# First FFN of a two-layer trunk: 18 of its 22 gate and up pairs by one level of Strassen's scheme

## The reference

```python
def swiglu_ffn(x, norm_g, w_gate_up, w_down):
    gate, up = jnp.split(rms_norm(x, norm_g) @ w_gate_up, 2, axis=-1)
    return x + (jax.nn.silu(gate) * up) @ w_down
```

## Time and profile before

| | |
|---|---|
| median of three runs | 1491.09 us (1486.75 to 1492.95) |
| the profiled execution | 1486.6 us, span of its instructions 1484.9 us |
| TensorE matmuls / weight loads | busy 1431.6 us (96%) / 1336.6 us (90%) |
| VectorE, ScalarE, GpSimd | busy 879.9 us (59%), 646.4 us (44%), 159.4 us (11%) |
| granted TensorE clock, mean | 0.991 of 2.4 GHz |
| read from HBM | 134.73 MB |

### The profile page before, as it was taken

One profiled execution on the slowest core, in us unless ns is written; L12 is line 12 of the kernel. 1 busy time (PEld: TensorE's weight loads), 2 busy tenths in 40 slices (PEclk: granted clock), 3 DMA queues, 4 the chain that ended last, 5 costly groups with the idle time before them and its releaser, 6 DMA issues.

```text
span 1484.9 us, 29208 instructions
## 1 busy us (share of the span) xinstructions
PE 1431.6 (96%) x11504; PEld 1336.6 (90%) x11504; DVE 879.9 (59%) x1562; ACT 646.4 (44%) x1086; POOL 159.4 (11%) x194
## 2 busy tenths in 40 slices
PE   7999988898999999999999999999998999999998
PEld 6999987887899999999999967755698999999998
DVE  6887556667984444443223426466577999997222
ACT  5444532333443443433222364556655655555111
POOL 1000022202630000000111000253110000000000
PEclk9999989999999999999999999999999999999999
DMA  5222200002444223233322322265521333233322
GB/s 219 86 85 85 74 12 30 29 30 87 156 149 141 86 85 99 86 98 106 92 83 97 113 62 85 74 196 159 171 85 58 98 102 105 93 113 107 91 91 83
DMA packets 48588, 144.79 MB, mean 98 GB/s; under 512 B 6912, under 2 KB 16224, under 8 KB 47344
## 3 DMA queue, kind: packets, MB, share of 16 engines
q1 hardware_dynamic: 42048, 118.57, 25.0%
q0 software_dynamic: 6160, 20.79, 4.7%
q10 hardware_dynamic: 288, 4.19, 0.7%
HBM read 134.73 MB, written 7.76 MB: 96 GB/s over the span
## 4 chain that ended last, share of the span: by engine, by line
PE 81%; DVE 10%; issue 5%; ACT 3%; DMA 1%; DVEq 0%; ACTq 0%; POOLq 0%
PE PS L610 67%; PE PS L1317 4%; PE PS L1318 4%; PE PS L1319 4%; DVE arena L2164 2%; ACT arena L1825 1%; PE PS L1143 1%; DVE arena L2327 1%; DVE mx L2602 1%; DVE arena L2154 0%; DVE arena L2159 0%; ACT wsplit L1376 0%; ACT wsplit L1450 0%; DVE wsum L1996 0%; DVE arena L2379 0%
## 5 line engine op out<-in xcount | busy, mean ns | idle before, releaser
L610 PE MATMUL PS<-xnh,wsplit 128*128 128x260 f32 x2496 | 410.8, 285 | 12.8 <-DVE wsplit L1932 12.4
L610 PEld LDWEIGHTS PS<-xnh,wsplit 128*128 128x128 f32 x2496 | 346.7, 190 | 15.7 <-DVE wsplit L1932 13.1
L1376 ACT ACTIVATE wsplit<-wring 128x1024 fp32r<-128x1024 f32 x132 | 136.3, 1033 | 326.0 <-PE PS L610 323.7
L1932 DVE TENSOR_TENSOR wsplit<-wring,wsplit 128x1024 fp32r<-128x1024 f32 x132 | 157.1, 1190 | 172.9 <-ACT wsplit L1376 172.8
L610 PE MATMUL PS<-xnl,wsplit 128*128 128x260 f32 x1248 | 252.2, 284 | 0.0
L610 PEld LDWEIGHTS PS<-xnl,wsplit 128*128 128x128 f32 x1248 | 193.3, 189 | 0.0
L610 PE MATMUL PS<-arena 128*128 128x128 f32 (+9 forms) x1104 | 170.9, 322 | 13.1 <-DVE arena L2327 8.6
L1317 PE MATMUL PS<-movh,wsplit 128*128 128x260 f32 x616 | 176.2, 286 | 6.3 <-ACT rinv L1496 2.8
L610 PEld LDWEIGHTS PS<-arena 128*128 128x128 f32 (+2 forms) x1104 | 134.3, 191 | 48.3 <-issue 30.1
L1319 PE MATMUL PS<-movh,wsplit 128*128 128x260 f32 x616 | 174.3, 283 | 0.0
L1318 PE MATMUL PS<-movl,wsplit 128*128 128x260 f32 x616 | 174.2, 283 | 0.0
(11 more groups left out here) (451 smaller groups left out, 2245.6 us busy)
## 6 DMA issues: line engine op xcount, KB each, us to landing
wring<-in_w_gu SPq DMA_DIRECT2D x88, 512.0 KB, 3.5
wring<-in_w_dn SPq DMA_DIRECT2D x32, 512.0 KB, 3.5
wring<-in_w_proj SPq DMA_DIRECT2D x28, 512.0 KB, 3.5
wring<-in_w_dn SPq DMA_DIRECT2D x16, 384.0 KB, 3.1
wring<-in_w_outa SPq DMA_DIRECT2D x8, 512.0 KB, 4.0
wring<-in_w_inc SPq DMA_DIRECT2D x8, 512.0 KB, 3.5
wring<-in_w_uq SPq DMA_DIRECT2D x8, 512.0 KB, 4.6
wring<-in_w_outc SPq DMA_DIRECT2D x8, 512.0 KB, 4.3
```

Of the source, the lines that this page charges most:

```text
L610: return pe.matmul(out, lhsT, rhs, start=start, stop=stop)
L1376: act.activation(dst[:, 0:w], wring[slot(stage, u)][:, 0:w], ACT.Copy).then_inc(s('w_hi'), 1)
L1932: tt(wl[:, 0:w], wring[slot(stage, u)][:, 0:w], wh[:, 0:w].bitcast(F32), ALU.subtract).then_inc(s('w_split'), 1)
```

## The change

The first FFN gets the scheme of the second for 18 of its pairs. The functions of the second FFN (`block_high`, `block_low`, `block_sum`, `gate_up_pair`, the body of the pair loop, the tiles of the down projection) take the layer as an argument `l` and are shared; `PAIRS` is 18 pairs in layer 0 and 22 in layer 1, and `pair_past` and `mov_past` shift layer 1's semaphore counts behind layer 0's. What is new:

- Four pairs stay plain (`PLAIN = 4`). While they run, the token side is made from `x`: ScalarE scales all eight chunks of `x` again (`gained`), VectorE makes four sums per pair of chunks in three operations (`sums0`), and the sums are split (`sums_high`, `sums0_low`). The three products that take `x` itself use the split that the plain pairs use (`moving`).
- The up tile isn't multiplied by the root any more, in the plain pairs either; the product of the first FFN carries one factor of the root too few, and it is multiplied in behind the down projection (`down_added`).
- Hidden tiles are kept whole (`hidden`), and six of them (`NEARLY`) are split within the pairs 6 to 11; tiles 6 to 21 are split behind the last pair, since their high halves lie where the sums of the token side lie. TensorE waits for each hidden tile by itself in the first down tile.
- The weight file of layer 0 has its chunks in the order `K_ORDER`, as layer 1's has; the plain tiles pick their chunk by it.
- The pairs of layer 0 are written out on ScalarE and VectorE and loop over four on TensorE; the down tiles of layer 0 are written out too.

```diff
+PAIRS = (KF - PLAIN, KF)
+BLK, NKEEP, NEARLY = 4 * 128, 10, 6
+T_LOW = {0: (0,), 1: (1,), 3: (2,), 4: (3,)}
+        low0 = (split("hid0l0", 2 * KD, 12), split("hid0l1", 44, KF - 12))
+        high0 = (split("hid0h0", 54, NEARLY), split("hid0h1", 28, KF - NEARLY))
+        def moving(l, q, m):
+            if l:
+                return tuple(v[:, 0, :] for v in mov(q, MOVES[m]))
+            if m in (0, 3, 5):
+                k, cols = 2 * q + (m > 0), slice(0, HALF) if m < 5 else slice(HALF, TOK)
+                return xnh[:, k, cols], xnl[:, k, cols]
+            at_ = 4 * q + {1: 0, 4: 1, 2: 2, 6: 3}[m]
+            return tmh[:, at_, :], tml[:, at_, :]
...
         def slot_freed(stage, i, u):
             if stage == 'gu1':
-                return past('blk_split', i * (2 * NB) + (6, 7, 13, 14)[u])
+                return pair_past(1, 'blk_split', i * (2 * NB) + (6, 7, 13, 14)[u])
+            if stage == 'gu0' and i >= PLAIN // 2:
+                return pair_past(0, 'blk_split', (i - PLAIN // 2) * (2 * NB) + (6, 7, 13, 14)[u])
...
-            split_gemm('gu0', xnh, xnl, norm=1)
-            pe.wait_ge(s('hid_ready'), sum(DOWN[:2]))
-            split_gemm('dn0', hidh, hidl)
+            split_gemm('gu0', xnh, xnl, norm=1, end=PLAIN // 2)
+            head = 4 if PAIRS[0] % 4 == 0 else 2
+            for j in range(head):
+                gate_up_pair(0, j, j, opening=j == 0)
+            with pe.Fori(0, (PAIRS[0] - head) // 4) as i:
+                for e in range(head, head + 4):
+                    gate_up_pair(0, i * 4 + e, e)
+            down_tiles(0)
...
+                gained(0)
+                gained(1)
+                norm_root(1)
...
+                for v in range(2 * PLAIN):
+                    j = v // 2
+                    act.wait_ge(gemm_ready[v % 2], TBASE['gu0'] + j + 1)
+                    if v + 2 < 2 * PLAIN:
+                        high('gu0', (v + 2) // 4, (v + 2) % 4)
+                    else:
+                        block_high(0, 2 * (v % 2))
+                        block_high(0, 2 * (v % 2) + 1)
+                    if v % 2 == 0:
+                        act.wait_ge(tile_taken[0], TBASE['gu0'] + j + 1)
+                        act.activation(sgate[:, j % 2, :], sgate[:, j % 2, :], ACT.Silu).then_inc(s('silu_ready'), 1)
+                    if v < 4:
+                        sums_high(v)
+                        if v < 2:
+                            gained(v + 2)
+                gate_up_pairs(0)
+                rest_high(0, 6, 7)
+                high('dn0', 0, 1)
+                rest_high(0, 8, 9, 10, 11, 12)
+                act.preload_act_table_set(LN_EXP)
...
+            def down_added(l, tile, temp):
+                p = tile % 2
+                dve.wait_ge(gemm_ready[p], TBASE[f'dn{l}'] + tile // 2 + 1)
+                st(tt(two(temp), bank2(2 * p), two(rinv[:, R_NORM[2 * l + 1] % 2, :]), ALU.mult))
+                st.sync()
+                st(tt(xres[:, tile, :], xres[:, tile, :], temp, ALU.add), tile_taken[p])
+            def sums0(q):
+                g, x = gx[q % 2], tx0[q % 2]
+                dve.wait_ge(*mov_past(0, 'mov_hi', {0: 2, 1: 4, 2: 7, 3: 10}[q]))
+                if q >= 2:
+                    dve.wait_ge(*mov_past(0, 'mov_split', q - 1))
+                tt(x[:, 0:2, :], g[:, 1:4:2, :], g[:, 0:2, :], ALU.subtract).then_inc(later('mov_sum'), 1)
+                dve.wait_ge(*mov_past(0, 'mov_sum', 3 * q + 1))
+                tt(x[:, 2, :], g[:, 3, :], x[:, 0, :], ALU.subtract).then_inc(later('mov_sum'), 1)
+                dve.wait_ge(*mov_past(0, 'mov_sum', 3 * q + 2))
+                tt(x[:, 3, :], g[:, 2, :], x[:, 2, :], ALU.subtract).then_inc(later('mov_sum'), 1)
+            def first_ffn():
+                sums0(0)
+                sums0(1)
+                dve.wait_ge(s('rinv_ready'), R_NORM[1] + 1)
...
+                for v in range(2 * PLAIN):
+                    j = v // 2
+                    dve.wait_ge(gemm_ready[v % 2], TBASE['gu0'] + j + 1)
+                    if v % 2 == 0:
+                        if j >= 2:
+                            dve.wait_ge(tile_taken[1], TBASE['gu0'] + j - 1)
+                        tt(two(sgate[:, j % 2, :]), bank2(0), two(root), ALU.mult).then_inc(tile_taken[0], 1)
+                    else:
+                        dve.wait_ge(s('silu_ready'), j + 1)
+                        tt(two(hidden(0, j)[0]), two(sgate[:, j % 2, :]), bank2(2), ALU.mult).then_inc(tile_taken[1], 1)
+                    if v == 2 * PLAIN - 2:
+                        block_sum(0, 0, 0)
+                    if v + 2 < 2 * PLAIN:
+                        low('gu0', (v + 2) // 4, (v + 2) % 4)
+                    else:
+                        block_low(0, 2 * (v % 2))
+                        if v % 2 == 0:
+                            block_sum(0, 0, 1)
+                        else:
+                            block_sum(0, 0, 2)
+                        block_low(0, 2 * (v % 2) + 1)
+                    for q in T_LOW.get(v, ()):
+                        sums0_low(q)
+                        if q < 2:
+                            sums0(q + 2)
+                dve.wait_ge(tile_taken[1], TBASE['dn0'])
+                gate_up_pairs(0)
+                rest_low(0, 6, 7)
+                low('dn0', 0, 1)
+                rest_low(0, 8, 9, 10, 11, 12)
...
-        if l:
-            gu = f[f'w_gu{l}'].reshape(-1, 128, KD, 128)[:, :, K_ORDER]
-            f[f'w_gu{l}'] = np.ascontiguousarray(gu).reshape(-1, 128, KD * 128)
+        gu = f[f'w_gu{l}'].reshape(-1, 128, KD, 128)[:, :, K_ORDER]
+        f[f'w_gu{l}'] = np.ascontiguousarray(gu).reshape(-1, 128, KD * 128)
```

## The result

The changed kernel took 1468.66 us (median of four runs, 1465.83 to 1469.80) against 1490.28 us before: ratio 0.9854, 95% interval 0.9828 to 0.9879. The prediction said 1467 us, in a range of 1458 to 1479.

What follows compares the result with a forecast made beforehand. TensorE, without gaps in the first FFN's gate and up tiles, was taken as the bound. A 23.8 us gain less 0.3 and 1.0 gave 22.5 net: 1464.1 from the profile, 1468.6 from the median, forecast 1467, range 1458 to 1479.

Steps and rivals of the forecast that it cites:

- Eighteen pairs, 183.9 us: First FFN's gate and up: twelve pairs at 10.05 us and six with a hidden split at 10.55, against 207.7 us before.
- 0.3 for the opening: Start of the seven-product pairs: blocks waiting for copies with one product of cover cost 0.3 us, bounds 0 and 3.7.
- Moving sums, cost 0: Token-side sums during the plain pairs: 10.0 us on ScalarE and 11.0 on VectorE fit; cost 0, without cover 0.8 us.
- Start of the down projection, 1.0 us: First down projection: TensorE waits for late-split hidden tiles, mainly tile 13; 1.0 us, bounds 0 and 2.5.
- The step on the table load: ScalarE's queue at the down projection's start: a 1.28 us activation table load stands ahead of third weights and tile 13.
- Norm root, cost 0: Behind the first down projection: one more VectorE operation of 0.70 us for each of eight tiles is hidden; cost 0.
- Net 22.5 us in the FFN: First FFN: gain of 23.8 us from the pairs, less 0.3 for the opening and 1.0 for the down projection's start.
- Rival 1: Seven-product pairs: VectorE's added durations set the pace, 10.20 us or 10.89 with a hidden split; 1472.4 us, chance 0.09.
- Rival 2: Seven-product pairs: weight loads keep their present rhythm, so pairs stay at 11.54 us; 1492 us, chance 0.04.
- Rival 3: Seven-product pairs: late bank hand-overs by ScalarE or VectorE make a pair 13.25 us; 1523 us, chance 0.05.
- That no other stretch changes by over 2 us: Outside the first FFN: the prediction called itself wrong if another stretch changed by over 2 us.
- The whole time: Whole kernel: 1464.1 us from the profiled execution, 1468.6 from the median; forecast 1467 us, chance 0.82.

Runs made afterwards that it cites:

- run 2: Changed kernel with VectorE's residual (low part) of each early hidden tile moved to the front of the next pair, both FFNs; first gate and up stretch 232.18 us against 232.19.
- run 5: Changed kernel, both FFNs: ScalarE's rounding of early hidden tiles moved behind the fifth block, VectorE's residual one pair later at its old slot; gate and up stretch 231.52 us.
- run 6: Changed kernel, both FFNs: ScalarE's rounding of early hidden tiles behind the fifth block, VectorE's residual at the next pair's front; stretch 230.09 us, whole 1460.19 us.
- run 4: Changed kernel with two plain pairs instead of four, so twenty seven-product pairs; gate and up stretch 231.25 us against 232.19.
- run 3: Changed kernel with ScalarE's activation table load moved behind the high halves of hidden tiles 13 to 21; first down projection 126.99 us against 127.56.
- run 7: Changed kernel without the multiplication by the norm root behind the first down projection; that projection 127.58 us.
- run 1: Changed kernel with GpSimd instead of VectorE making the residuals of the first FFN's six early hidden tiles; gate and up stretch 234.67 us against 232.19.
- run 8: Changed kernel measured again without an edit, on another chip; 1467.91 us, ratio to before 0.9874.

## Why the prediction was right, step by step

- *Eighteen pairs, 183.9 us, and 0.3 for the opening.* Measured 184.20 us, of it about 0.2 at the opening, ahead of the first pair's last product. The two rhythms were 10.10 and 10.45 us where 10.05 and 10.55 were taken from the second FFN: 12 x 0.05 more and 6 x 0.10 less, which cancel. That the sum came out to 0.1 us is luck; why the fast pairs took 0.05 us more here no run shows. What made the slow pairs slow was told wrongly: the prediction put it down to VectorE alone, as the waits show it. Runs 2, 5 and 6 showed ScalarE's rounding to be the larger of two causes, either enough. The number didn't suffer, because the pairs from which it was read had both causes too. A wait names what came last, here VectorE, not who made that one late.
- *Moving sums, cost 0.* The four plain pairs took 47.99 us; before, 255.72 - 207.7 = 48.0. Right: the split of the fourth tile ended at 444.92 and TensorE began that tile at about 446.0, 1.1 us later (forecast 0.5). One reading on the way was wrong: the four plain pairs fill 48 us and not the 55.14 us whose busy times the prediction took; the room was smaller than it said, but enough. With two pairs (run 4) it was not: 1.6 us of waiting for the last remainder.
- *Start of the down projection, 1.0 us.* Measured 0.84, of it 0.60 at tile 13, 10.25 us behind the start. VectorE gave the tile when forecast (T+10.3, forecast T+10.2); TensorE wanted it later (about T+9.8, forecast T+9.3). The step on the table load was shown by run 3.
- *Norm root, cost 0.* Shown by run 7.
- *Net 22.5 us in the FFN.* Measured 23.53 - 0.84 = 22.7. The parts close: 18 x 12 = 216 matmuls fewer at 0.120 us are 25.9 us; six slow pairs took back 2.1 us (6 x 0.35), the opening 0.2 and the start of the down projection 0.8.
- *Rival 1* (VectorE's durations added, 10.20 us a pair) failed: the rhythm without a hidden split was 10.10, and operations of 0.69 us started 0.60 to 0.61 us apart (542.88 and 543.48 in run 1's rows). The Trainium skill, "VectorE: DVE Perf Modes", section "The DRAIN you can't avoid", says first that the next operation doesn't start until the pipe is empty, and then that one that isn't held starts earlier; these rows agree with the second and not with the first. *Rival 2* failed: 102 GB/s came in, where weights at the old rhythm are 91, with TensorE busy 183.64 of 184.20 us. *Rival 3* failed: the waits list none for TensorE in all eighteen pairs; the gaps of 0.25 us ahead of the last product of the six slow pairs, and the one at the opening, were all.
- *That no other stretch changes by over 2 us* was wrong. The stretch behind the FFN was 8.1 us longer in the first profile. That is why the profiled executions lie only 16.8 us apart (1484.9 and 1468.1 us of span) where the FFN gained 22.7; an earlier start (426.67 against 428.86) gave 2.2 back, and that isn't the change either: the changed kernel again started at 425.14, the kernel before again at 427.07. Runs with the same mean clock, 0.988, take clock out: before 1488.20 and 1489.41 us, changed 1465.83 and 1465.18, 22.4 to 24.2 apart, though not on one chip. The medians, 21.6 us apart here and 18.9 in run 8, hold both.
- *The whole time.* From the median the sum gave 1468.6 us, and 1468.66 was measured; from the profile it gave 1464.1, and the profiled execution took 1469.8. The first agreement is in part luck, since the stages that the sum doesn't look at moved by 2 to 8 us between executions. What the prediction got right is the FFN.

## What to carry to other kernels

When one FFN of a kernel already runs the scheme that another is to get, take the time of a repeat from it, separately for each kind of repeat, and add only what the start and the end cost. When two engines each have a small piece of extra work in the same repeat, move both before judging either, since the larger one hides the other. Judge an edit worth a few us by its own stretch in two traces: a stage that nobody touched moved by 8 us with the clock.

## What had not been expected of the hardware

Most of the clock's fall lies in the attention layer, where pages of keys come in. Three stretches of 10 us there in the changed kernel:

```profile
926.42:936.42 10.00, 9.65 (x56) 8.56 (x56) 7.60 (x32) 3.12 (x10) 4.60 (x10) 0.80 0.27 72
936.42:946.42 10.00, 9.66 (x79) 6.13 (x78) 1.39 (x5) 3.70 (x10) 4.87 (x10) 0.50 0.49 138
946.42:956.42 10.00, 10.00 (x65) 5.86 (x65) 4.30 (x13) 4.29 (x11) 6.09 (x12) 0.85 0.65 190
```

and the matching ones before:

```profile
951.32:961.32 10.00, 9.67 (x87) 8.39 (x87) 7.60 (x32) 4.87 (x13) 4.57 (x10) 1.00 0.27 71
961.32:971.32 10.00, 9.65 (x90) 5.21 (x90) 4.37 (x13) 3.96 (x13) 7.16 (x14) 0.83 0.76 218
971.32:981.32 10.00, 10.00 (x82) 6.08 (x79) 5.48 (x17) 5.99 (x18) 4.75 (x10) 1.00 0.65 186
```

The clock was granted at its lower level, 1.2 of 2.4 GHz, for a whole stretch (0.50), and in parts of its neighbours; before, only in part of one. Up to its fall in the changed kernel, at 932.3, TensorE did the same work in both kernels, matmuls of 8 to 512 columns. Here the changed kernel fell 5.7 us behind (the same ScalarE operation starts 163.72 us into the stretch at 950.14, and 158.00 us into it before). The rest came later, where the clock was down in part of each of these stretches and at 1.00 in the matching ones before:

```profile
1042.00:1052.00 10.00, 8.49 (x64) 4.88 (x65) 4.14 (x10) 5.80 (x14) 0.00 (x0) 0.83 0.40 141
1052.00:1062.00 10.00, 10.00 (x81) 9.83 (x77) 3.38 (x10) 2.04 (x8) 0.00 (x0) 0.83 0.21 71
1062.00:1072.00 10.00, 10.00 (x72) 10.00 (x72) 3.95 (x7) 4.11 (x7) 0.75 (x1) 0.83 0.10 37
```

Behind them it was 9.8 us behind (ScalarE's split at 1067.50, at 1082.58 before), of which the kernel before lost 1.7 at a fall of its own, at 1124 to 1134. The clock's mean over a run follows the time closely: before had 1484.32 us at 0.992 and 1492.89 at 0.985. The changed kernel's eight runs lay at 0.985 to 0.988, while the kernel before had 0.985 to 0.992. It isn't the denser FFN as such: run 4, with two pairs more in the new form, had 0.988 to 0.992. Run 1, 2.5 us slower in its FFN, had a lower ratio to before (0.9843) than the changed kernel (0.9854, and 0.9874 in run 8); its runs had 0.989 to 0.992. Why kernels with the changed kernel's timing were granted less (runs 2 and 7 too, 548.04 and 550.62 us in that stretch) stays open; run 3, whose way to that stretch was only 0.6 us shorter, had 544.84 there, and no run moved that stage alone in time.

The other two were GpSimd holding up VectorE (run 1, 1.12 us instead of 0.69), and VectorE starting operations of 0.69 us every 0.60 to 0.61 us when they waited for nothing (542.88 and 543.48 in run 1's rows), which is why a pair fitted into 10.10 us where its durations add up to 10.20.
